# mLSTM chunks of a hybrid decoder step: decode outer products taken in turn with the state increments, and gate spreads in turn with the key-query products

## The chip, the cores and the metric

The kernel runs on one core of a Trainium2 chip. The metric is the device time of one execution in microseconds (us). The kernel before was timed in three runs; a change of under 0.3%, some 8 us, is not told from no change.

## The reference, cut to what matters

The kernel is one inference step of a two-layer decoder trunk for a prompt of 1024 tokens and 8 decode samples of one token. Layer 0 runs an S5 scan and, beside it, an mLSTM with 4 heads of width 128; layer 1 is a sparse attention. The change lies in the mLSTM alone. For the prompt it is computed chunk by chunk, with a state C (128 x 128 and a 129th column for n) per head:

```python
s = jnp.einsum('bhtd,bhsd->bhts', qj, kj) * w_intra
num = jnp.einsum('bhts,bhsd->bhtd', s, vj) + w_inter[..., None] * jnp.einsum('bhtk,bhkv->bhtv', qj, c)
c_new = decay[..., None, None] * c + jnp.einsum('bhs,bhsk,bhsv->bhkv', w_end, kj, vj)
```

`w_intra` and `w_inter` are exponentials of cumulated log gates. For each decode sample the same step has one token, so that its addition to the state is one outer product k v per head. All matmuls of the stage are f32.

## The kernel before, in words

The stage is the function `phase_ml_chunks`, and it stands between the stage that prepares gates (`phase_ml_front`) and the output projection. The prompt is cut into 8 chunks (NMC) of 128 tokens (MC), counted from 0; there are also 8 decode samples, and chunk c carries sample c along. Each engine has its own program, written out by hand, and they meet at semaphores alone: there is no planner, and the order of the lines is the order on the engine.

What TensorE does for chunk c, in this order:

- `gains(c)`: first the decode products of the sample before (`apply`, L1848, moving operand of one column), then the **state increments** (L1858): for each of 4 heads the scaled keys, 128 rows of weights, times the values with a column of ones, 129 columns.
- `outer(c)`: the **decode outer products** (L1841): for each head the lone key of sample c (8 rows of weights, all but one zero) times the 8 samples' values.
- `inputs(c + 1)`: the **spreads** (L1804): for each head a selector of 4 rows, which lays a row of log gates over 128 partitions; the **key-query products** (L1809), 128 rows of weights; then four key transposes (L1816) and four value transposes (L1820), into the bank that held the outer products.
- `numbers(c)`: for each head the products of probabilities and values (L1871) and, from chunk 1 on, of queries and state (L1873), in turn, adding up in the same place.
- `turn(c - 1)`: four transposes (L1882) of the finished rows of the chunk before.

`inputs(0)` runs once ahead of the loop, and after it the samples' rows are turned (L1826 to L1835).

The other engines follow. ScalarE waits for the spreads (`pe_a`), takes two sets of exponentials (L1910, L1913), waits for the transposes, copies the values (L1916) and scales the keys (L1918, signal `act_c`). GpSimd masks the first exponentials (L1936), multiplies the second with the queries (L1944) and makes the lone key of a later sample (`alone`, L1929, signal `key_alone`). VectorE updates the state from the increments (`advance`, L1969, after `pe_d`), the decode state from the outer products (`update`, L2020, after `outer_done`), weighs the key-query products (`weigh`, L1958, after `pe_b`), divides (L1977 to L1988) and gates (L1993). SyncE stages later chunks and stores the decode states; its program is not touched.

Two waits matter below. `turn(c - 1)` waits for `act_c` of chunk c + 1, since its bank held the keys. `inputs(c + 1)` waits with its value transposes for VectorE's `update(c)` (`dve_d`).

Of the kernel before, what the change touches and what calls it, by code (L numbers as in the profile page):

```python
# [51 lines left out]
MH = 4  # L52
DH = 128
MC = 128
# [1696 lines left out]
def phase_ml_chunks(m):  # L1751

    nc = m.nc
    s = m.ml
    scale = DH ** -0.5
    ps_a, ps_s, ps_v, ps_k = m.ps[0], m.ps[1], m.ps[2], m.ps[3]
    W = DH + 1
    heads = lambda bank: bank[:].rearrange("p (h t) -> p h t", h=MH)
# [9 lines left out]
    with nc.Block() as block:  # L1768

        @block.sync  # L1770
        def _(sp):
            def stage(c):
                sp.dma_start(s.stage[c % 4], m.ml_dram[:, :, c * MC:(c + 1) * MC]).then_inc(loads[c % 4].sem, 16)

            stage(2)
            stage(3)
            for b in range(B):
                sp.dma_start(s.c_smp[b], m.ins["state_mlstm_c"][b].rearrange("h k v -> k h v")).then_inc(m.page_in[b].sem, 16)
            sp.wait_ge(m.act_e.sem, m.act_e.at(1))
            sp.dma_start(m.outs["s_n"].rearrange("b h k -> (b h) k"), s.n_rows[0:B * MH, 1]).then_inc(m.stored.sem, 16)  # L1780
            for c in range(NMC):
                sp.wait_ge(m.dve_d.sem, m.dve_d.at(c + 1))
                sp.dma_start(m.outs["s_c"][c].rearrange("h k v -> k h v"), s.c_smp[c]).then_inc(m.state_out.sem, 16)
                if c + 4 < NMC:
                    sp.wait_ge(m.dve_e.sem, m.dve_e.at(c + 1))
                    stage(c + 4)
            sp.wait_ge(m.dve_b.sem, m.dve_b.at(NMC))
            sp.dma_start(m.outs["p_c"].rearrange("b h k v -> k (b h) v"), s.c_state[NMC % 2][:, :, 0:DH]
                         ).then_inc(m.stored.sem, 16)
            sp.wait_ge(m.act_e.sem, m.act_e.at(2))  # L1790
            sp.dma_start(m.outs["p_n"].rearrange("b h k -> (b h) k"), s.n_rows[0:MH, 0]).then_inc(m.stored.sem, 16)
            sp.wait_ge(m.state_out.sem, m.state_out.at(16 * B))
            sp.wait_ge(m.stored.sem, m.stored.at(48))

        @block.tensor
        def _(pe):
            def inputs(c):
                load = loads[c % 4]
                x = s.stage[c % 4]
                pe.wait_ge(load.sem, load.at(16 * (c // 4 + 1)))  # L1800
                if c >= 1:
                    pe.wait_ge(m.act_d.sem, m.act_d.at(c))
                for h in range(MH):
                    last = nc.tensor.matmul(heads(ps_a)[:, h], s.sel[:, h], s.a[:, c * MC:(c + 1) * MC], start=True, stop=True)  # L1804
                last.then_inc(m.pe_a.sem, 1)
                if c >= 1:
                    pe.wait_ge(m.dve_a.sem, m.dve_a.at(c))
                for h in range(MH):
                    last = nc.tensor.matmul(heads(ps_s)[:, h], x[:, 4 + h], x[:, h], start=True, stop=True)  # L1809
                last.then_inc(m.pe_b.sem, 1)  # L1810
                if c >= 1:
                    pe.wait_ge(m.act_c.sem, m.act_c.at(c))
                if c >= 3:
                    pe.wait_ge(m.dve_e.sem, m.dve_e.at(c - 2))
                for h in range(MH):
                    nc.tensor.transpose(heads(ps_k)[:, h], x[:, 4 + h], m.ident[:])  # L1816
                if c >= 1:
                    pe.wait_ge(m.dve_d.sem, m.dve_d.at(c))
                for h in range(MH):
                    last = nc.tensor.transpose(heads(ps_v)[:, h], x[:, 8 + h], m.ident[:])  # L1820
                last.then_inc(m.pe_c.sem, 1)

            def sample_rows():
                pe.wait_ge(m.smp_keys.sem, m.smp_keys.at(1))
                for h in range(MH):
                    nc.tensor.transpose(v_bank[0:B, h * DH:(h + 1) * DH], v[:, h], m.ident[:])  # L1826
                    nc.tensor.transpose(k_bank[0:B, h * DH:(h + 1) * DH], s.kw[:, h], m.ident[:])
                pe.wait_ge(m.norms_in.sem, m.norms_in.at(16))
                nc.tensor.transpose(n_bank[:, 0:B * MH], s.n_rows[0:B * MH, 0], m.ident[0:B * MH, 0:B * MH]
                                    ).then_inc(m.smp_turned.sem, 1)  # L1830

            def sample_norms():
                pe.wait_ge(m.smp_rows.sem, m.smp_rows.at(1))
                nc.tensor.transpose(v_bank[0:B * MH, 0:P], s.nt.rearrange("p b h -> p (b h)"), m.ident[:])
                nc.tensor.matmul(k_bank[:, 0:MH * B], m.ones[:], s.prod.rearrange("p h b -> p (h b)"),  # L1835
                                 start=True, stop=True).then_inc(m.smp_turned.sem, 1)

            def outer(b):
                pe.wait_ge(m.key_alone.sem, m.key_alone.at(b + 1))
                for h in range(MH):  # L1840
                    last = nc.tensor.matmul(heads(ps_v)[:, h], s.k_one[b % 2][:, h], s.v_smp[:, h], start=True, stop=True)  # L1841
                last.then_inc(m.outer_done.sem, 1)

            def apply(b):
                pe.wait_ge(m.dve_d.sem, m.dve_d.at(b + 1))
                for h in range(MH):
                    at = h * B + b
                    last = nc.tensor.matmul(y_smp[:, at:at + 1], s.c_smp[b][:, h], q[:, h, b:b + 1], start=True, stop=True)  # L1848
                return last

            def gains(c):
                pe.wait_ge(m.act_b.sem, m.act_b.at(c + 1))
                pe.wait_ge(m.act_c.sem, m.act_c.at(c + 1))
                if c >= 1:
                    pe.wait_ge(m.dve_b.sem, m.dve_b.at(c))
                    apply(c - 1)
                for h in range(MH):
                    last = nc.tensor.matmul(gain(h), s.k_tok[c % 2][:, h], s.v_ext[c % 2][:, h], start=True, stop=True)  # L1858
                last.then_inc(m.pe_d.sem, 1)

            def numbers(c):
                pe.wait_ge(m.dve_a.sem, m.dve_a.at(c + 1))
                if c == 0:
                    pe.wait_ge(m.act_e.sem, m.act_e.at(1))
                    pe.wait_ge(m.smp_sum.sem, m.smp_sum.at(1))
                if c >= 1:
                    pe.wait_ge(m.pool_b.sem, m.pool_b.at(c))
                    pe.wait_ge(m.dve_b.sem, m.dve_b.at(c))
                    pe.wait_ge(m.dve_c.sem, m.dve_c.at(c))
                for h in range(MH):  # L1870
                    last = nc.tensor.matmul(num(h), s.probs[c % 2][:, h], s.v_ext[c % 2][:, h], start=True, stop=(c == 0))  # L1871
                    if c >= 1:
                        last = nc.tensor.matmul(num(h), s.q_part[c % 2][:, h], s.c_state[c % 2][:, h], start=False, stop=True)  # L1873
                last.then_inc(m.pe_e.sem, 1)

            def turn(c):
                pe.wait_ge(m.dve_c.sem, m.dve_c.at(c + 1))
                pe.wait_ge(m.act_c.sem, m.act_c.at(min(c + 3, NMC)))
                if c >= 1:
                    pe.wait_ge(m.dve_e.sem, m.dve_e.at(c))  # L1880
                for h in range(MH):
                    last = nc.tensor.transpose(heads(ps_k)[:, h], s.h_tok[c % 2][:, h], m.ident[:])  # L1882
                last.then_inc(m.turned.sem, 1)

            inputs(0)
            sample_rows()
            sample_norms()
            pe.wait_ge(m.pool_c.sem, m.pool_c.at(1))
            for c in range(NMC):
                gains(c)  # L1890
                outer(c)
                if c + 1 < NMC:
                    inputs(c + 1)
                numbers(c)
                if c >= 1:
                    turn(c - 1)
            pe.wait_ge(m.dve_b.sem, m.dve_b.at(NMC))
            apply(B - 1).then_inc(m.applied.sem, 1)
            nc.tensor.transpose(ps_a[0:MH, 0:P], s.c_state[NMC % 2][:, :, DH], m.ident[:]).then_inc(m.mean_part.sem, 1)
            turn(NMC - 1)  # L1900
# [1574 lines left out]
```

## Time and profile before

| what | value |
|---|---|
| median of 3 runs | 2732.41 us (2730.5 to 2737.38) |
| the profiled execution | 2744.11 us |
| its span, first to last instruction | 2742.3 us |
| granted TensorE clock, mean over the span | 0.962 |
| from L1804 of the first inputs to the end of the stage | some 380.8 to 465 us |

Times in the trace are us from the span's start. PE is TensorE, PEld its weight loads, DVE VectorE, ACT ScalarE, POOL GpSimd. Matmuls are pipelined: a record lasts longer than the distance to the next one, so that distances between starts tell the pace, and the busy time of PE does not. PEclk is the granted clock: 1.00 is 2.4 GHz, 0.50 is 1.2 GHz. The form of a matmul is written as rows*columns of the weights, then rows x columns of the moving operand; an f32 matmul leaves two records.

### The profile page before, as it was taken

Reading aid. Unit: us, or ns where it says so; the run is one execution under the profiler, and the core shown is the slowest. Engines: PE = TensorE matmul, PEld = TensorE weight load, DVE = VectorE, ACT = ScalarE, POOL = GpSimd, SP = SyncE. Lnnn points to the kernel's source line nnn. Section 1 sums busy time; section 2 is a strip of 40 time slices with the busy share of each in tenths; the row PEclk is TensorE's granted clock in tenths of the full one; section 3 lists DMA queues with packets and bytes.
Section 4 is the critical chain, followed back from the end, with each engine's and each line's share of the span. In section 5 each row is a group of like instructions: output and inputs, shape, how many; then the busy total and the mean of one; then the engine's idle time right before and its main releaser. Section 6 shows DMA issues by size and latency. Waiting matters only on the chain. (4 is left out here: it accounts for less than half of the span.)

```text
span 2742.3 us, 43365 instructions
## 1 busy us (share of the span) xinstructions
PE 2645.1 (96%) x16469; PEld 2529.0 (92%) x16469; DVE 1098.3 (40%) x2395; ACT 566.8 (21%) x1010; POOL 1196.7 (44%) x1520
## 2 busy tenths in 40 slices
PE   7899999999999999999898997999999999999998
PEld 7899878999999999999757996888999999999998
DVE  6958656242121121124259967554342121121223
ACT  3010243121010010111044533443120010010112
POOL 5544222665455554557302311000665455554552
PEclk8999988999999999999879997999999999999999
DMA  6525535111111111111303225202111111111111
GB/s 205 101 80 98 168 94 164 45 46 48 46 45 53 42 45 52 46 46 43 111 10 93 92 64 173 74 1 86 40 46 50 47 44 51 43 49 46 46 46 70
DMA packets 291412, 188.45 MB, mean 69 GB/s; under 512 B 41030, under 2 KB 281290, under 8 KB 290522
## 3 DMA queue, kind: packets, MB, share of 16 engines
q1 hardware_dynamic: 265590, 178.54, 21.6%
q10 hardware_dynamic: 25700, 8.32, 2.5%
q8 instruction: 72, 1.18, 0.2%
q14 instruction: 50, 0.41, 0.1%
HBM read 151.84 MB, written 34.98 MB: 68 GB/s over the span
## 5 line engine op out<-in xcount | busy, mean ns | idle before, releaser
L521 POOL TENSOR_TENSOR w_hi<-w_raw,ones 128x256 fp32r<-128x256 f32 x720 | 619.9, 892 | 1281.8 <-PE ps L532 1154.9
L524 POOL TENSOR_TENSOR w_lo<-w_raw,w_hi 128x256 fp32r<-128x256 f32 x720 | 535.5, 774 | 25.6
L532 PE MATMUL ps<-out_x_hi,w_hi 128*128 128x344 f32 x1920 | 409.1, 322 | 6.9 <-DVE out_x_lo L2109 6.9
L532 PE MATMUL ps<-next_hi,w_hi 128*128 128x344 f32 x1920 | 414.9, 325 | 0.0
L532 PE MATMUL ps<-next_lo,w_hi 128*128 128x344 f32 x1920 | 409.8, 322 | 0.0
L532 PE MATMUL ps<-out_x_lo,w_hi 128*128 128x344 f32 x1920 | 408.6, 321 | 0.0
L532 PE MATMUL ps<-next_hi,w_lo 128*128 128x344 f32 x1920 | 407.1, 321 | 0.0
L532 PE MATMUL ps<-out_x_hi,w_lo 128*128 128x344 f32 x1920 | 406.6, 320 | 0.0
L2134 DVE TENSOR_TENSOR resid<-ps,resid 128x344 f32 (+1 forms) x240 | 108.9, 510 | 706.5 <-PE ps L532 706.5
L532 PEld LDWEIGHTS ps<-out_x_hi,w_hi 128*128 128x128 f32 x1920 | 324.6, 189 | 7.4 <-issue 7.4
L532 PEld LDWEIGHTS ps<-next_lo,w_hi 128*128 128x128 f32 x1920 | 327.2, 190 | 0.0
L532 PEld LDWEIGHTS ps<-out_x_lo,w_hi 128*128 128x128 f32 x1920 | 326.2, 190 | 0.0
L532 PEld LDWEIGHTS ps<-next_hi,w_hi 128*128 128x128 f32 x1920 | 324.8, 190 | 0.9
L532 PEld LDWEIGHTS ps<-next_hi,w_lo 128*128 128x128 f32 x1920 | 322.1, 189 | 0.0
L532 PEld LDWEIGHTS ps<-out_x_hi,w_lo 128*128 128x128 f32 x1920 | 321.1, 188 | 0.0
L2247 DVE SCALAR_TENSOR_TENSOR relu<-ps,inv_rms 128x344 f32<-128x344 f32 x192 | 87.1, 510 | 522.7 <-PE ps L532 520.4
L2219 ACT ACTIVATE relu<-relu 128x1032 f32<-128x1032 f32 x64 | 68.4, 1069 | 1099.4 <-DVE relu L2247 1099.4
L532 PE MATMUL ps<-in_x_hi,w_hi 128*128 128x344 f32 x480 | 115.8, 351 | 10.0 <-POOL w_lo L524 4.3
L532 PE MATMUL ps<-in_x_lo,w_hi 128*128 128x344 f32 x480 | 105.2, 329 | 0.0
L532 PE MATMUL ps<-in_x_hi,w_lo 128*128 128x344 f32 x480 | 104.8, 328 | 0.0
L532 PEld LDWEIGHTS ps<-in_x_hi,w_hi 128*128 128x128 f32 x480 | 83.2, 197 | 18.6 <-issue 14.0
L2238 DVE TENSOR_TENSOR out_x_lo<-relu,out_x_hi 128x1032 f32 (+1 forms) x64 | 90.0, 1406 | 19.3 <-issue 12.9
(550 smaller groups left out, 2778.2 us busy)
## 6 DMA issues: line engine op xcount, KB each, us to landing
w_raw<-in_w_up SPq DMA_DIRECT2D x64, 512.0 KB, 4.0
w_raw<-in_w_down SPq DMA_DIRECT2D x64, 512.0 KB, 4.0
w_raw<-in_w_in SPq DMA_DIRECT2D x36, 512.0 KB, 4.6
resid_spill<-resid SPq DMA_DIRECT2D x2, 4128.0 KB, 13.7
ml_inputs<-in_ring SPq DMA_DIRECT2D x16, 516.0 KB, 3.0
resid<-resid_spill SPq DMA_DIRECT2D x4, 2064.0 KB, 7.5
w_raw<-in_w_out SPq DMA_DIRECT2D x16, 512.0 KB, 4.3
keys<-in_cache_k SPq DMA_DIRECT2D x64, 128.0 KB, 2.0
```

Source lines behind the costliest of these rows:

```text
L521: m.nc.gpsimd.tensor_tensor(parts(hi[:, k]), x[:, k], one, ALU.mult)
L524: last = m.nc.gpsimd.tensor_tensor(parts(lo[:, k]), x[:, k], hi[:, k], ALU.subtract)
L532: ins = nc.tensor.matmul(out[c], parts(w), parts(x[:, token_cols(c)]), start=first and n == 0, stop=last and n == 2)
L2134: last = nc.vector.tensor_tensor(x, m.ps[3 * slot + c][:, 0:CH], x, ALU.add)
L2219: nc.scalar.activation(m.relu[slot], m.relu[slot], ACT.Square)
L2238: nc.vector.tensor_tensor(flat(parts(m.h_lo[:, bass.ds(u, 1), :])), m.relu[slot], flat(m.h_hi[:, bass.ds(u, 1), :]), ALU.subtract).then_in ...
L2247: last = nc.vector.scalar_tensor_tensor(m.relu[slot][:, token_cols(c)], m.ps[3 * slot + c][:, 0:CH], 0.0, m.inv_rms[:, token_cols(c)], ALU ...
```

## The change

The increments of a head and its decode outer product are now issued in turn, inside `gains`, and the wait for the lone key stands ahead of both; `outer` is gone. In `inputs` the key-query product of a head and its spread are issued in turn, with both waits ahead. Each of the four signals still goes out with the last instruction of its kind. Nothing is added or left out, and no other engine's program changes.

```diff
@@ inputs(c)
                 if c >= 1:
                     pe.wait_ge(m.act_d.sem, m.act_d.at(c))
-                for h in range(MH):
-                    last = nc.tensor.matmul(heads(ps_a)[:, h], s.sel[:, h], s.a[:, c * MC:(c + 1) * MC], start=True, stop=True)
-                last.then_inc(m.pe_a.sem, 1)
-                if c >= 1:
                     pe.wait_ge(m.dve_a.sem, m.dve_a.at(c))
                 for h in range(MH):
-                    last = nc.tensor.matmul(heads(ps_s)[:, h], x[:, 4 + h], x[:, h], start=True, stop=True)
-                last.then_inc(m.pe_b.sem, 1)
+                    wide = nc.tensor.matmul(heads(ps_s)[:, h], x[:, 4 + h], x[:, h], start=True, stop=True)
+                    last = nc.tensor.matmul(heads(ps_a)[:, h], s.sel[:, h], s.a[:, c * MC:(c + 1) * MC], start=True, stop=True)
+                wide.then_inc(m.pe_b.sem, 1)
+                last.then_inc(m.pe_a.sem, 1)
@@
-            def outer(b):
-                pe.wait_ge(m.key_alone.sem, m.key_alone.at(b + 1))
-                for h in range(MH):
-                    last = nc.tensor.matmul(heads(ps_v)[:, h], s.k_one[b % 2][:, h], s.v_smp[:, h], start=True, stop=True)
-                last.then_inc(m.outer_done.sem, 1)
-
@@ gains(c)
                     apply(c - 1)
+                pe.wait_ge(m.key_alone.sem, m.key_alone.at(c + 1))
                 for h in range(MH):
                     last = nc.tensor.matmul(gain(h), s.k_tok[c % 2][:, h], s.v_ext[c % 2][:, h], start=True, stop=True)
+                    alone = nc.tensor.matmul(heads(ps_v)[:, h], s.k_one[c % 2][:, h], s.v_smp[:, h], start=True, stop=True)
                 last.then_inc(m.pe_d.sem, 1)
+                alone.then_inc(m.outer_done.sem, 1)
@@ the loop
                 gains(c)
-                outer(c)
                 if c + 1 < NMC:
```

## Rows read from the trace of the kernel before

**Rows 1.** The page's first part: busy time, share of the span, instructions.

```profile
PE 2645.1 (96%) x16469; PEld 2529.0 (92%) x16469; DVE 1098.3 (40%) x2395; ACT 566.8 (21%) x1010; POOL 1196.7 (44%) x1520
```

**Rows 2.** Chunks 1 to 6: length, busy PE PEld DVE ACT POOL, PEclk, DMA, GB/s.

```profile
401.71:456.59 54.88, 54.69 (x410) 52.91 (x410) 30.49 (x105) 22.71 (x78) 17.92 (x20) 0.88 0.37 106
```

**Rows 3.** Timeline of TensorE in chunk 3: start, us from first start to end, instruction.

```profile
420.91 1.14 PE L1858 MATMUL ps<-ml_work 128*128 128x129 f32 x8
421.98 1.15 PE L1841 MATMUL ps<-ml_work 8*128 8x128 f32 x8
422.98 1.05 PE L1804 MATMUL ps<-ml_rows 4*128 4x128 f32 x8
423.96 1.16 PE L1809 MATMUL ps<-ml_ahead 128*128 128x128 f32 x8
424.95 0.60 PE L1816 MATMUL ps<-ident,ml_ahead 128*128 128x128 f32 x4
...
425.83 0.39 PE L1871 MATMUL ps<-ml_work 128*128 128x129 f32 x2
426.05 0.39 PE L1873 MATMUL ps<-ml_work 128*128 128x129 f32 x2
...
427.87 0.63 PE L1882 MATMUL ps<-ident,ml_work 128*128 128x128 f32 x4
...
429.15 1.14 PE L1858 MATMUL ps<-ml_work 128*128 128x129 f32 x8
```

**Rows 4.** Timelines of hundredths of a microsecond at both changes of chunk 3.

```profile
421.78 0.27 PE L1858 MATMUL ps<-ml_work 128*128 128x129 f32 x1
...
422.19 0.38 PE L1841 MATMUL ps<-ml_work 8*128 8x128 f32 x2
...
423.76 0.27 PE L1804 MATMUL ps<-ml_rows 4*128 4x128 f32 x1
...
424.17 0.39 PE L1809 MATMUL ps<-ml_ahead 128*128 128x128 f32 x2
```

**Rows 5.** Timelines at half clock: one change in chunk 0, two groups of chunk 4.

```profile
395.20 0.42 PE L1804 MATMUL ps<-ml_rows 4*128 4x128 f32 x1
395.55 0.58 PE L1809 MATMUL ps<-ml_ahead 128*128 128x128 f32 x1
...
395.93 0.63 PE L1809 MATMUL ps<-ml_ahead 128*128 128x128 f32 x2
...
434.43 1.06 PE L1820 MATMUL ps<-ident,ml_ahead 128*128 128x128 f32 x4
435.28 0.64 PE L1871 MATMUL ps<-ml_work 128*128 128x129 f32 x2
```

**Rows 6.** Timeline of ScalarE in chunk 3, its first and last group.

```profile
424.07 1.15 ACT L1910 ACTIVATE ml_work<-ps,s_small 128x128 f32<-128x128 f32 x4 [5.46 <-PE ps L1804]
...
426.56 1.22 ACT L1918 ACTIVATE ml_work<-ps,s_small 128x128 f32<-128x128 f32 x4
```

**Rows 7.** TensorE alone in three stretches: length, busy, granted clock, DMA share, GB/s.

```profile
405.50:408.80 3.30, 3.30 (x18) 0.50 0.00 0
...
415.80:419.00 3.20, 3.20 (x17) 0.50 0.99 295
419.20:432.70 13.50, 13.40 (x114) 1.00 0.37 105
```

**Rows 8.** Timelines of all engines: chunks 0, 2 and 7, first inputs, first lone key.

```profile
380.77 2.04 PE L1804 MATMUL ps<-ml_rows 4*128 4x128 f32 x8 [3.16 <-PEq L290]
...
390.53 2.03 POOL L1929 TENSOR_TENSOR ml_work<-ml_work,ident 8x512 f32<-8x512 f32 x2 [5.84 <-DVE s_small L2004]
...
390.77 1.14 PE L1858 MATMUL ps<-ml_work 128*128 128x129 f32 x8
...
411.31 1.14 PE L1858 MATMUL ps<-ml_work 128*128 128x129 f32 x8
...
456.59 1.14 PE L1858 MATMUL ps<-ml_work 128*128 128x129 f32 x8
```

## The prediction

> **What bounds it now.** The span's sections are read first: TensorE is busy for 2645 of 2742 us [rows 1], and so tells little by itself. What the change touches is the mLSTM chunk phase, and the second view sums that stretch: between the first matmul of chunk 1's increments and that of chunk 7's (chunks count from 0), 54.88 us, TensorE is busy for 54.69, VectorE for 30.5, ScalarE for 22.7, GpSimd for 17.9 [rows 2]. So TensorE's order sets the time of a chunk. The third view is one chunk in order of time [rows 3]: each f32 matmul leaves two records, so four heads make 8. Chunk 3 runs from 420.91 to 429.15, 8.24 us. Two readings matter. The state products (L1871) and the intra-chunk products (L1873) already alternate, and a pair of records still takes 0.22 us (425.83 to 426.05), 0.11 a record. Alternation of lines and PSUM addresses costs nothing as such; all of these have 128 rows of weights. And a run of 8 at 0.11 should take 0.89 us, but the increments take 1.07 and the products L1809 0.99.
>
> **Where the extra sits** is seen in single records [rows 3, 4]. The last increment (128 rows) starts at 421.78, the first decode outer product (8 rows) at 421.98, the second at 422.19: 0.41 us where two records take 0.22. The same when it goes back: the last spread (4 rows) at 423.76, the first key-query product at 423.96, the second at 424.17, again 0.41. So **a change between few-row and 128-row weights costs 0.19 us**, in either direction. From the 8-row outer products to the 4-row spreads there is no such step: the run L1804 begins 1.00 us after L1841, and of that 0.19 is the change at L1841's own front and the rest its eight records. Waits that are already met cost nothing either: the transposes L1816 wait for two semaphores and L1871 for one to four, at 0.11. At the half clock a record takes 0.213 us (434.43 to 435.28 for four), and a change 395.20 to 395.55 to 395.93, 0.73 for two records, that is 0.30 dearer than 0.43 [rows 5].
>
> **The change, part by part.** No instruction is added or removed; the DMAs, GpSimd, VectorE and ScalarE code stay.
>
> 1. *Alternation.* The increments and outer products go wide, few, wide, few: 7 changes inside where there was 1. The key-query products and spreads likewise: 1 into them, 7 inside, 1 out to the transposes. A chunk with both has 16 changes against 2, so 14 more; the last chunk has 8 against 2, the first inputs ahead of the loop 8 against 1. In all 7 x 14 + 6 + 7 = 111 more. At full clock that is 111 x 0.19 = 21.1 us. A lower end: nothing. I take the whole price, since it is the same at every one of the changes in the four cases looked at.
>
> 2. *The spreads' signal comes later.* ScalarE starts its exponentials when the spreads end (424.07) and is done with the scaled keys at 426.56 + 1.22 = 427.78; the turn of the previous chunk (L1882) waits for that and starts at 427.87 [rows 3, 6]. From the last spread's start, 423.76, that is 4.11 us. TensorE now fills them with L1809, the transposes and L1871/L1873 and is short of work for only 0.25 us (425.83 + 16 x 0.112 = 427.62, the turn at 427.87). After the change L1809 is no longer behind the signal: 0.11 + 0.19 + 8 x 0.11 + 16 x 0.112 = 2.97, so TensorE waits 1.14 us, 0.88 more than now, in a chunk at full clock. At half clock it has 0.21 + 0.30 + 24 x 0.213 = 5.6 us of work there, and nothing waits. What is queued behind this wait is the turn, the decode products L1848 and the next increments; VectorE's normalising of the turned rows waits for it too, and isn't on the path.
>
> 3. *The increments' signal comes later*, after 16 records and 7 changes (3.3 us, before 1.1). VectorE then does 1.12 us of state update and 1.12 of decode update; the value transposes wait for the second, and lie another 3.3 us and four transposes behind. Covered by about 1 us, and without that cover it would cost what VectorE is late. The wait for the previous weighting, now ahead of the spreads, is met a chunk earlier: free.
>
> 4. *Chunk 0's key.* GpSimd makes the first lone key from 390.53 on, 1.03 us each [rows 8]. The increments now wait for it, where they ran from 390.77 in its shade: about 0.8 us, once. Later keys are made a chunk ahead and are free.
>
> 5. *The clock.* In this phase the granted clock is at 1.2 GHz in short stretches. Here TensorE is busy in all of 405.50 to 408.80 and 415.80 to 419.00, with the clock at 0.50, and in 419.20 to 432.70, with it at 1.00 [rows 7]; the same view has two more half-speed stretches, from 432.8 and 443.1. All four begin inside L1809 or the transposes L1816, after both few-row runs (1.98 us of them) went by; none begins behind the 28 wide records that end a chunk, and all four end during those. So what goes before a fall is few-row work. In the alternated stretch a wide pair and a few-row pair with their two changes take 0.83 us at full clock, of which 0.22 is wide records, 0.22 few-row ones and 0.38 stall, and this goes on for 6.6 us, where few-row work now lasts 1.98. I expect a fall in every chunk, and a return only in the wide stretch behind it.
>
> Of TensorE's clock the Trainium skill ("TensorE: Matmul & The Clock Gate", The HAM clock gate) says that it follows how busy the PE was. Taken as the profile's busy share it would stay up here and the sum would be some 22 us; the rows above, busy throughout and yet at half speed, speak against that reading.
>
> **The sum.** A chunk wholly at full clock: 8.24 + 14 x 0.19 + 0.88 = 11.8 us. Wholly at half: 68 records (16 + 16 + 8 + 16 + 4 + 8) x 0.213 + 16 x 0.30 = 19.3. Stepping through, the clock falls inside the alternation and rises inside the transposes and L1871/L1873, so part of these, the turn and the next increments go at full clock: I take the middle, 15.5. Seven chunks 108.5 us, where now 456.59 - 390.77 = 65.8 [rows 8]: +42.7. The last chunk, 6 changes, partly at half clock: +2.5. The inputs ahead of the loop run at half clock (L1804, 2.04 us for 8 records at 380.77): 7 x 0.30 = +2.1. The key: +0.8. Together +48 us. The profiled execution took 2744.1 us (its span 2742.3), 11.7 above the median 2732.4 of the runs; nothing in the phase explains that difference, and I put the sum on the median: 2780.
>
> **Rivals.**
> - *Changes cost, the clock holds as now.* 21.1 + 7 x 0.88 less what half-clock chunks hide of it, + 0.8, less the falls that vanish (four of 1.36, the difference of a 9.60 us chunk such as 411.31 to 420.91 and 8.24): +20 to +28. For it: chunks 3 and 6 ran the same records and kept the full clock, so the falls hang on more than the few-row runs. Against: the alternated stretch has over three times as much of what goes before a fall.
> - *Half clock throughout.* 7 x 19.3 - 65.8 + 6 = +75. Against: each wide stretch at half speed now brings the clock back.
> - *Not slower: the weight loads hide.* If few-row and 128-row weights, taken in turn, load beside the other's columns, a change is free. The place is each LDWEIGHTS of the alternated pairs; the chunk then is 1.79 + 1.79 of alternation, 4.0 to the turn and 1.28 of turn and decode, 8.9 us, 62 for seven: with the key -3 us if the clock then never falls, +3 if it falls in four chunks as now; take 0. It decides while a change costs under some 0.05 us (16 x 7 x 0.05 = 5.6 on top of +3). For it: in the runs of now each change stands alone, its first record after a run. Against: the first change and the change back cost the same 0.19.
>
> The Trainium skill says in "TensorE: Matmul & The Clock Gate", Part 3, that a weight load overlaps matmuls in flight only when the row groups differ. Read loosely it favours this case, no change of time; but 4 rows and 8 rows share a group and pass at 0.11 here, and 8 against 128 rows is where the rows stall.
>
> **Chances.** Forecast (+38 to +62) 0.70; clock holds 0.18; half throughout 0.05; hidden loads 0.06; a gain over 0.3% 0.01. 0.3%, or 8 us, is about what a measurement tells from no change. Slower 0.93, same 0.06, faster 0.01. The range takes the forecast's and most of the clock rival's: 2752 to 2792, which leaves out half throughout, hidden loads and the outer edges.
>
> **What would show it.** Pitches in the alternated stretch of 0.11, 0.20, 0.21 at full and 0.21, 0.35, 0.37 at half clock; increments plus outer products 3.1 to 5.5 us for 16 records instead of 2.07; an idle of about 1 us before the turn (L1882) only in chunks whose L1871/L1873 run at full clock; granted clock over the phase near 0.65 to 0.75 instead of 0.88; other phases unchanged. I am wrong if alternated records keep 0.11, if the clock stays near 0.88, or if VectorE's update ends behind the key transposes.

## The result, and the profile after

The changed kernel took 2779.76 us in the median of six runs (2767.48 to 2785.88), where the kernel before took 2734.89 in six (2730.5 to 2740.26). The ratio is 1.015, with a 95% interval of 1.013 to 1.0169: 36 to 46 us slower (the two medians lie 45 us apart). The profiled execution took 2779.69 us, its span is 2777.9.

Busy time of the engines in the page's first part, for comparison with [rows 1]:

```profile
PE 2677.1 (96%) x16469; PEld 2546.5 (92%) x16469; DVE 1105.4 (40%) x2395; ACT 564.5 (20%) x1010; POOL 1199.2 (43%) x1520
```

TensorE gains 32 us of busy time with the same 16469 records and VectorE 7; ScalarE and GpSimd move by under 3. Busy time by stretch, all engines, chunks 1 to 6 as in [rows 2], and below it one chunk late in the phase (columns: length, then PE PEld DVE ACT POOL busy, PEclk, DMA share, GB/s):

```profile
408.92:494.20 85.28, 85.28 (x411) 70.30 (x410) 31.30 (x108) 22.13 (x78) 18.62 (x21) 0.72 0.24 68
439.29:453.01 13.72, 13.72 (x70) 11.37 (x70) 5.23 (x19) 3.69 (x13) 2.90 (x3) 0.75 0.33 97
```

The stretch went from 54.88 to 85.28 us, TensorE is still without a gap in it, and the granted clock went from 0.88 to 0.72. TensorE's weight loads, busy for 52.91 of 54.88 us before, are now busy for 70.30 of 85.28: the loads leave 15 us open where they left 2, though the matmul records leave none. TensorE's timeline shows it, first at the start of the phase, then in that late chunk (chunk 3), to set beside [rows 3, 8]:

```profile
379.65 0.77 PE L1805 MATMUL ps<-ml_ahead 128*128 128x128 f32 x2 [3.16 <-PEq L290]
...
385.41 1.11 PE L1814 MATMUL ps<-ident,ml_ahead 128*128 128x128 f32 x4
...
392.57 0.77 PE L1851 MATMUL ps<-ml_work 128*128 128x129 f32 x2 [0.54 <-POOL ml_work L1923]
...
439.29 0.47 PE L1851 MATMUL ps<-ml_work 128*128 128x129 f32 x2
439.69 0.48 PE L1852 MATMUL ps<-ml_work 8*128 8x128 f32 x2
440.10 0.49 PE L1851 MATMUL ps<-ml_work 128*128 128x129 f32 x2
440.52 0.48 PE L1852 MATMUL ps<-ml_work 8*128 8x128 f32 x2
...
445.50 0.80 PE L1805 MATMUL ps<-ml_ahead 128*128 128x128 f32 x2
446.23 0.79 PE L1806 MATMUL ps<-ml_rows 4*128 4x128 f32 x2
446.95 1.11 PE L1814 MATMUL ps<-ident,ml_ahead 128*128 128x128 f32 x4
...
451.77 0.60 PE L1877 MATMUL ps<-ident,ml_work 128*128 128x128 f32 x4
...
453.01 0.47 PE L1851 MATMUL ps<-ml_work 128*128 128x129 f32 x2
```

From pair to pair it is 0.415 us at full clock (439.69 to 440.10 to 440.52) and 0.725 at half (445.50 to 446.95 for two pairs): the 0.22 + 0.19 and 0.43 + 0.30 of [rows 4, 5], at every change shown here. The granted clock by stretch, TensorE alone (length, busy, PEclk, DMA share, GB/s), beside [rows 7]:

```profile
410.40:424.00 13.60, 13.60 (x48) 0.50 0.00 0
424.10:430.80 6.70, 6.70 (x42) 1.00 0.35 98
430.90:437.60 6.70, 6.70 (x29) 0.50 0.32 95
437.70:444.50 6.80, 6.80 (x43) 1.00 0.31 91
```

From chunk 2 on the clock alternates between the two levels: it falls in the alternation (here at 430.9 and 444.6, among L1805 and L1806) and returns near the end of L1866/L1868. In chunks 0 and 1 it is at half for far longer. The transfers do not explain it. Before, the half-clock stretch from 415.80 had a DMA share of 0.99 and the full-clock one behind it 0.37 [rows 7]; here the stretch of 13.60 us at half clock has none at all, and the later ones have 0.31 to 0.35 at either level.

Where the time went, by the starts of the first increments. Seven chunks took 65.82 us before and take 494.20 - 392.57 = 101.63, each in turn 16.35, 16.65, 13.72, 13.72, 13.73, 13.73 and 13.73 us. The first inputs took 384.61 - 380.77 = 3.84 and take 385.41 - 379.65 = 5.76. The first increment starts 1.21 us after the samples' L1832 (391.36), 0.27 before. From the first increment of the last chunk to the output projection's first matmul it is 13.08 us, 12.00 before; the last chunk stays at full clock. That is 35.8 + 1.9 + 0.9 + 1.1 = 39.7 us more in the phase, and the two profiled spans differ by 35.6, since other parts of these two executions took 4 us less.

### The profile page after: what moved, and what is told of

It reads as the page before. It is cut to its first block and busy times, and to the rows that moved or that the text cites. A ratio compares the mean times of both kernels' runs of the same rounds, so it can differ in the third digit from the quotient of the medians.

```text
span 2777.9 us, 43366 instructions
## 1 busy us (share of the span) xinstructions
PE 2677.1 (96%) x16469; PEld 2546.5 (92%) x16469; DVE 1105.4 (40%) x2395; ACT 564.5 (20%) x1010; POOL 1199.2 (43%) x1520
## 5 line engine op out<-in xcount | busy, mean ns | idle before, releaser
L2232 DVE TENSOR_TENSOR out_x_lo<-relu,out_x_hi 128x1032 f32 (+1 forms) x64 | 90.2, 1409 | 19.2 <-issue 12.9
```

Of the source, the lines that this page charges most:

```text
L2232: nc.vector.tensor_tensor(flat(parts(m.h_lo[:, bass.ds(u, 1), :])), m.relu[slot], flat(m.h_hi[:, bass.ds(u, 1), :]), ALU.subtract).then_in ...
```

## The experiments

Of the kernel before, each set of runs has its own on the same chip; the ratios are to those. Single executions of one kernel here lie up to 30 us apart, so a few us are told by the traces and hardly by the medians.

### One alternation at a time

The gains as changed, with the two runs of `inputs` as before (the wait between the two runs is back as well, and isn't shown):

```diff
-                for h in range(MH):
-                    wide = nc.tensor.matmul(heads(ps_s)[:, h], ...)
-                    last = nc.tensor.matmul(heads(ps_a)[:, h], ...)
+                for h in range(MH):
+                    last = nc.tensor.matmul(heads(ps_a)[:, h], ...)
+                last.then_inc(m.pe_a.sem, 1)
+                for h in range(MH):
+                    last = nc.tensor.matmul(heads(ps_s)[:, h], ...)
+                last.then_inc(m.pe_b.sem, 1)
```

> Only the increments and decode outer products are taken in turn; spreads and key-query products stay in runs. Theory A (each change of weight rows costs 0.19 us at full and 0.30 at half clock, and few-row stretches bring the clock down): 8 changes a chunk against 2, so 6 more, 1.1 us at full clock, and a fall of the clock in every chunk, so that a chunk takes 10.8 to 11.5 us where before it took 9.4 in the mean: with the wait for chunk 0's key (+0.9) and the last chunk (+1.2) +12 to +17 us on before. Rival B (changes cost, the clock falls as often as before): 48 x 0.19 + 0.9 = +10. Rival C (the whole loss is in one of the two alternations): near 0 or near +40.

Measured: 2756.31 us median of 10, ratio 1.0063 (1.0042 to 1.0085), +17 us.

The other half is the kernel before with the changed `inputs` (signals and waits as in the change, not shown):

```diff
-                for h in range(MH):
-                    last = nc.tensor.matmul(heads(ps_a)[:, h], ...)
-                for h in range(MH):
-                    last = nc.tensor.matmul(heads(ps_s)[:, h], ...)
+                for h in range(MH):
+                    wide = nc.tensor.matmul(heads(ps_s)[:, h], ...)
+                    last = nc.tensor.matmul(heads(ps_a)[:, h], ...)
```

> Only the key-query products and spreads are taken in turn; increments and outer products stay in runs. Theory A: 10 changes a chunk against 2, so 8 more, 1.5 us at full clock, the signal for ScalarE later, and the clock at half for a part of every chunk: a chunk 11.2 to 12.3 us, with the first inputs (+1.9) +15 to +22 us on before. Rival B (clock as before): 7 x 8 x 0.19 + 2 = +13, up to +18 if ScalarE's later start adds 0.88 a chunk at full clock. Rival C: near 0 or near +40. The two halves together below the whole (+40) speak for A, since the clock is lost only where the few-row stretch is long.

Measured: 2758.44 us median of 6, ratio 1.0066 (1.0046 to 1.0087), +18 us. Both alternations cost, by like amounts, and rival C is out. The sum of the halves is +35 against +41 with intervals of some 6 us each way, so whether they add up can't be told, and that part of the expectation gives no verdict. Whether the clock falls more often, which tells theory A from rival B, is read from the traces: seven chunks of the gains-only kernel and, below, of the inputs-only kernel (TensorE alone):

```profile
388.15:472.72 84.57, 83.70 (x464) 0.74 0.33 89
```

```profile
392.65:482.77 90.12, 89.74 (x465) 0.70 0.28 80
```

Before it was 65.82 us at 0.84. Rival B, changes at their price and the clock as before, gave +10 and +13 to +18. The gains alone exceed it (+12 to +23 by the interval), with a clock 0.10 lower than before. The time of the inputs alone lies at B's upper end and doesn't decide; there the clock, 0.14 lower, speaks against B. The chunks are longer than theory A had them, 12.1 us in the mean for the gains (10.8 to 11.5 expected) and 12.9 for the inputs (11.2 to 12.3), and the seven of each took 18.8 and 24.3 us more than before, together more than the 35.8 of the whole change, not less. The profiled execution of the inputs-only kernel was 10 us above its median, so of it only the direction is used.

### Half as many changes

The changed kernel, in turn by two heads:

```diff
-                for h in range(MH):
-                    last = nc.tensor.matmul(gain(h), ...)
-                    alone = nc.tensor.matmul(heads(ps_v)[:, h], ...)
+                for g in range(0, MH, 2):
+                    for h in (g, g + 1):
+                        last = nc.tensor.matmul(gain(h), ...)
+                    for h in (g, g + 1):
+                        alone = nc.tensor.matmul(heads(ps_v)[:, h], ...)
```

and the same in `inputs`.

> The changed kernel, but in turn by two heads: two wide matmuls, two few-row ones, twice; the same for products and spreads. 8 changes a chunk instead of 16, 6 more than before instead of 14; the signals as late as in the changed kernel. Theory A: 6 x 0.19 = 1.14, up to 0.88 of waiting for ScalarE, and one fall of the clock a chunk: a chunk 10.9 to 12 us, with the key +11 to +19 us on before. Rival (the loss follows the late signals and not the number of changes): +30 to +40. Rival B (changes alone at full price): 6 x 7 x 0.19 + 2 = +10.

Measured: 2762.42 us median of 4, ratio 1.0103 (1.0069 to 1.0136), +28 us (19 to 37). That is above the +11 to +19 expected and below the +30 to +40 of the rival, whose lower part the interval reaches, so the time alone doesn't decide. The trace of it has chunks of 14.79, 15.48, 10.71, 10.67, 10.28, 13.70 and 10.28 us. Two of them, 10.28 us each, ran wholly at full clock: 8.24 + 6 x 0.19 + 0.9, the terms of theory A. What it missed are the chunks that run nearly all at half clock, the first two above all. At full clock the cost follows the number of changes; how often the clock stays down is not foreseen by counting them.

### How many rows make the stall

The order of the changed kernel with other operands for the few-row matmuls, which leaves out the right outer products and spreads; the numbers that come out are others. With 96 rows:

```diff
-                    last = nc.tensor.matmul(heads(ps_a)[:, h], s.sel[:, h], s.a[:, c * MC:(c + 1) * MC], start=True, stop=True)
+                    last = nc.tensor.matmul(heads(ps_a)[:, h], x[0:96, 4 + h], m.ident[0:96, :], start=True, stop=True)
-                    alone = nc.tensor.matmul(heads(ps_v)[:, h], s.k_one[c % 2][:, h], s.v_smp[:, h], start=True, stop=True)
+                    alone = nc.tensor.matmul(heads(ps_v)[:, h], s.k_tok[c % 2][0:96, h], s.v_ext[c % 2][0:96, h, 0:DH], start=True, stop=True)
```

> The order of the changed kernel, but the few-row matmuls have weights of 96 rows: the outer product takes rows 0 to 95 of the scaled keys and values, the spread rows 0 to 95 of the keys and of an identity, so the decode states and the gates' exponentials are of other numbers. Theory A (row changes cost by themselves, and it is the few rows that bring the clock down): pairs of records stay at 0.41 us, the clock stays at 2.4 GHz, a chunk takes 11.8 us with about 1 us of waiting for ScalarE: +18 to +23 us on before. Rival D (the stalls bring the clock down, whatever the rows): +40 as the changed kernel. Rival E (96 rows overlap with 128, only 8 and 4 don't): near 0.

Measured: 2742.93 us median of 10, ratio 1.0023 (1.0001 to 1.0045), +6 us. TensorE's timeline of this kernel:

```profile
437.86 0.39 PE L1852 MATMUL ps<-ml_work 96*128 96x128 f32 x2
438.08 0.39 PE L1851 MATMUL ps<-ml_work 128*128 128x129 f32 x2
438.30 0.39 PE L1852 MATMUL ps<-ml_work 96*128 96x128 f32 x2
```

0.22 us a pair: there is no stall between 96 and 128 rows. Theory A had "a change of weight rows" as the cause; that was too wide, and rival E is right. Theory A also had the clock stay up here, and it didn't: it fell in five of the seven chunks, which took 10.15 to 10.60 us where the other two took 8.92, with neither few-row weights nor stalls in them. In the three falls looked at (chunks 2 to 4), it falls behind a wait of 1.16 to 1.21 us before the turn and the decode products of one column. With 64 rows (`[0:64]` in the place of `[0:96]`):

> The order of the changed kernel, few-row matmuls with weights of 64 rows (rows 0 to 63 of the scaled keys and values; of the keys and an identity; decode states and exponentials are of other numbers). Theory A, corrected by the run with 96 rows (which had no stall): a change stalls where the row counts are 64 or less against 128, as 64-row groups elsewhere in the trace of before do: pairs of records at 0.41 us; with more rows at work the clock falls less: a chunk 11.8 to 13.7 us, +18 to +35 on before. Rival D (the clock falls through stalls alone): as with 8 rows, +36 to +42. Rival H (only few rows stall, 64 do not): as 96 rows, 0 to +6.

Measured: 2779.06 us median of 4, ratio 1.0159 (1.0128 to 1.0191), +44 us. Its timeline from chunk 2's turn to chunk 3's, and then TensorE's busy time and clock over two whole chunks:

```profile
434.24 0.63 PE L1877 MATMUL ps<-ident,ml_work 128*128 128x128 f32 x4 [1.02 <-issue]
...
435.51 0.47 PE L1851 MATMUL ps<-ml_work 128*128 128x129 f32 x2
435.91 0.48 PE L1852 MATMUL ps<-ml_work 64*128 64x128 f32 x2
436.32 0.49 PE L1851 MATMUL ps<-ml_work 128*128 128x129 f32 x2
...
446.05 0.63 PE L1877 MATMUL ps<-ident,ml_work 128*128 128x128 f32 x4 [1.01 <-issue]
```

```profile
423.69:447.33 23.64, 21.61 (x138) 1.00 0.39 112
```

64 rows stall as 8 do, 0.41 us a pair, so rival H is out. The total (35 to 52 by the interval) came out at rival D's +36 to +42 and above A's +18 to +35: 8 and 16 times the rows did not keep the clock up, which speaks for the stalls rather than the few rows. It isn't decided, since this trace has three chunks of 11.82 us, with the same stalls and no fall, and others of 15.09 to 16.70. The three of 11.82 are what this run is good for: **the changed order wholly at full clock** (the changed kernel has no such chunk in its trace), with 16 changes and 1.02 us of waiting before the turn. The forecast had put that at 11.8 and 1.14. Against the 10.28 us of the kernel by twos, eight changes fewer, it is 1.54 us: 0.19 a change once more.

### No changes of rows at all

Lone keys, samples' values, selector and gate rows are padded with zeros to 128 rows; the numbers stay. First in the changed order:

```diff
-    s.ig, s.lf, s.b, s.mx, s.a, s.tmp, s.mask = (a.take(N, parts=MH) for _ in range(7))
-    s.sel = a.take(MH, P, parts=MH)
+    s.ig, s.lf, s.b, s.mx, s.a_all, s.tmp, s.mask = (a.take(N, parts=P if i == 4 else MH) for i in range(7))
+    s.sel_all = a.take(MH, P)
+    s.a, s.sel = s.a_all[0:MH], s.sel_all[0:MH]
...
-    s.v_smp = c.take(MH, DH, parts=B)
+    s.v_all = c.take(MH, DH)
+    s.v_smp = s.v_all[0:B]
...
-    s.k_one = [c.take(MH, DH, parts=B) for _ in range(2)]
+    s.k_all = [c.take(MH, DH) for _ in range(2)]
+    s.k_one = [x[0:B] for x in s.k_all]
```

with GpSimd memsets and two waits for them ahead, and the `_all` tiles in the two matmuls.

> The order of the changed kernel, with the lone keys, the samples' values, the selector and the gate rows padded with zeros to 128 rows, so that every matmul has 128 rows of weights and the numbers stay. Theory A: no stalls, pairs of records at 0.22 us, a chunk 8.9 us bound by ScalarE's chain behind the spreads, with 7 x (8.9 - 9.4) + 0.9 - 1: -6 to 0 us on before. Rival F (rows of zeros don't count for the clock): the clock still falls, chunk 10 to 12 us, +8 to +20. Rival G (alternation itself costs): +40.

Measured: 2742.6 us median of 10, ratio 1.0013 (0.9998 to 1.0029), +4 us (-1 to +8): the loss is all but gone, with the alternation kept, and rival G is out. It is above theory A's -6 to 0 and below rival F's +8 to +20; what A missed is that the clock still fell, as shown below. Then in the order of before:

> The order of the kernel before, with lone keys, samples' values, selector and gate rows padded with zeros to 128 rows. Theory A: the two row changes of a chunk vanish (2 x 0.19), ScalarE's chain takes 0.19 of that back, and the clock no longer falls in four of seven chunks (4 x 1.36): a chunk 8.05 us, together -5 to -9 us on before, of which the GpSimd memsets may take back 1 to 2. Rival F (rows of zeros don't count for the clock): only the changes go, -1 to -3. If 128 rows cost more than 4 or 8: slower.

Measured: 2729.22 us median of 12, ratio 0.9966 (0.9941 to 0.9992), -9 us, at the far end of the expected range. Two timelines, each from one chunk's numbers to its turn. The padded changed order:

```profile
429.11 0.39 PE L1872 MATMUL ps<-ml_work 128*128 128x129 f32 x2
430.64 0.63 PE L1881 MATMUL ps<-ident,ml_work 128*128 128x128 f32 x4 [1.15 <-issue]
```

The padded order of before, with its clock over seven chunks below (a separate view):

```profile
426.55 0.39 PE L1877 MATMUL ps<-ml_work 128*128 128x129 f32 x2
427.21 0.63 PE L1886 MATMUL ps<-ident,ml_work 128*128 128x128 f32 x4 [0.28 <-issue]
```

```profile
387.95:444.57 56.62, 53.30 (x467) 1.00 0.55 150
```

The first waits 1.15 us for ScalarE's keys before the turn, the second 0.28: 0.87 us, the price of the late signal by itself, forecast as 0.88. At full clock their chunks take 8.93 and 8.04 us (forecast 8.9 and 8.05). The padded order of before never leaves 2.4 GHz in the seven chunks of this execution, 56.62 us where they took 65.82. So matmuls with 4 or 8 rows of numbers did not bring the clock down where zeros fill them up to 128 and no change stalls, and rival F, which left the falls of before in place, is out. Whether it is the rows of zeros that keep the clock up or the missing stalls was not parted. The changed order, padded, still fell to half clock in four of its seven chunks (10.17 to 10.61 us), where the wait before the turn stands beside the decode products of one column.

### A version that beats both

Padded, and the next chunk's spreads, taken out of `inputs` with their waits into a function of their own, ahead of the decode products and increments:

```diff
             for c in range(NMC):
+                if c + 1 < NMC:
+                    spreads(c + 1)
                 gains(c)
                 outer(c)
```

> As the padded order of before, and the spreads of the next chunk go ahead of this chunk's decode products and increments, so that ScalarE starts some 2.7 us earlier against TensorE. Theory A with ScalarE's chain as the next limit: no wait before the turn, a chunk 7.7 us of pure records (68 x 0.112), -8 to -13 us on before. Rival (the chain behind the spreads isn't the limit at full clock): as the padded order alone, -5 to -9.

Measured: 2726.58 us median of 12, ratio 0.9954 (0.9937 to 0.9972), -13 us, the fastest here; that it beats the padded order alone can't be told, as the intervals overlap. Its chunks at full clock are no shorter, 8.03 to 9.25 us and not the 7.7 expected, so whatever it gains over the padded order isn't there; its profiled execution was 10 us above its median and can't say more. The chunk of 9.25 holds a wait of 1.01 us before the spreads, by the trace for the load of the next chunk's inputs: `spreads` took that wait along, though its matmuls read nothing that is loaded. ScalarE's chain is no longer what is waited for, but the wait has moved, which its timeline shows:

```profile
415.39 1.11 DVE L2035 SCALAR_TENSOR_TENSOR resid<-resid,s_small,ps 128x128 f32<-128x128 f32 x4
415.93 0.60 PE L1823 MATMUL ps<-ident,ml_ahead 128*128 128x128 f32 x4
...
416.56 0.66 PE L1827 MATMUL ps<-ident,ml_ahead 128*128 128x128 f32 x4
```

The value transposes (L1827) start 0.63 us after the key transposes where four records take 0.44: they wait for VectorE's decode update (415.39 + 1.11 = 416.50). It is the cover of step 3 of the forecast, used up here, where no spreads stand between the outer products and the transposes.

## Why the prediction was right

The time (2780 forecast, 2779.8 measured) agrees better than its terms do, and that closeness is luck. The difference was put at +48; by the ratio it is +41 (36 to 46), by the medians +45, and the kernel before came out 2.5 us above its first median in the later runs.

**Step 1, the alternation,** held: 0.19 us a change at full clock and 0.30 at half, at every change in the rows shown. That a change of rows is the cause held, with a correction: 4, 8 and 64 rows against 128 stall, and 96 against 128 is free. The case that weight loads hide had 0.06 and would have been right for 96 rows.

**Step 2, the spreads' late signal,** held in size (0.87 against 0.88, in the padded pair) and in its condition. In the changed kernel L1866/L1868 run mostly at half clock, and no wait stands before L1877: the term is hidden there, under work made longer by the slower clock.

**Step 3** held: in the changed kernel the value transposes follow the key transposes without a gap, VectorE is not late. The cover was put at about 1 us; in the full-clock chunk with 64 rows VectorE's update ends at 440.68 and the value transposes start at 442.65, 2.0 us later.

**Step 4:** 0.9 us for the first key, 0.8 forecast.

**Step 5, the clock,** held in kind: a fall in every chunk, a return in the wide stretch behind it, and 0.72 over chunks 1 to 6 where 0.65 to 0.75 was said. That the few-row, stalled stretch brings it down is supported by the padded order of before, which has the same matmuls in the same places, more rows and no fall. That it does so by its few rows, as "what goes before a fall is few-row work" has it, was not shown: rows and stalls weren't parted, 64-row weights, which stall alike, gave chunks of both kinds, and in the changed order with 96 rows and with padded rows it fell without either.

**The sum.** The step that was mis-sized is "I take the middle, 15.5": chunks took 14.5 in the mean, seven together +35.8 instead of +42.7. Five settled at 13.7 and two took 16.5; none was wholly at half clock, so the upper end, 19.3, was never reached. The full-clock end, 11.8, was exact (11.82 with 64 rows, the wait before the turn in it). With it the +35.8 divides: seven chunks at full clock are 7 x (11.82 - 8.24) = 25.1 us dearer, and the time lost to the clock grew from 65.82 - 7 x 8.24 = 8.1 to 101.63 - 7 x 11.82 = 18.9, 10.8 more. The last chunk and what follows it took 1.1 more instead of 2.5: "partly at half clock" did not come, and 6 x 0.19 = 1.1. The first inputs took 1.9 for 2.1.

On the two rules weighed. "TensorE: Matmul & The Clock Gate" of the Trainium skill, Part 3, has loads overlap matmuls in flight only when row groups differ. Here 4, 8 and 64 rows against 128 differ and stall, 96 against 128 overlap, and 128 against 128 overlap; the trace does not agree with it so read. The same page of the Trainium skill, The HAM clock gate, ties the clock to how busy the PE was: TensorE's busy share was 85.28 of 85.28 us at a clock of 0.72, so it isn't the profile's busy share that counts.

Open: why chunks 0 and 1 stay at half clock so much longer than the later ones, and what decides it in the kernels with pairs by two and with 64 rows. The reading of the falls in step 5 was of chunks 1 to 6. The kernel before has one more in chunk 0, at half clock from 391.9 to 398.5, which begins with the outer products themselves, behind a stretch in which TensorE mostly waited; so more than the few-row work decides.

## What to carry to other kernels

Look at single records where weights of few rows meet full ones: each such change cost 0.19 us at full clock, so few-row matmuls belong in one run, and where the tiles have room for it, padding the weights and moving operand with zeros to full rows removes the changes; here it kept the clock up as well (-0.34%, with 0.08% to 0.59% as its interval). When a signal is moved within a run of instructions, compare the chain behind it with the work that follows it at both levels of the clock: the wait is hidden at one and stands open at the other.

## What the runs showed of the hardware that was not expected

- Weights of 8, 4 and 64 rows next to 128 stall for 0.19 us a change at 2.4 GHz; 96 rows next to 128 don't (0.22 us a pair of records).
- A matmul whose operands are zeros but for 4 or 8 rows took the time of a few-row one, 0.11 us a record, and with all of them padded in the order of before the granted clock was 1.00 over 56.62 us.
- The same order of the same instructions gave chunks of 11.82 and of 16.70 us in one execution (64 rows), and 13.72 and 16.65 in the changed kernel; the longer ones are those with more time at half clock.
